# Attention inside a transformer block on TensorE: double units over two steps in place of single units over one

## The reference, cut to what is needed

```python
z = rms_norm(x, norm_mix_pre) @ w_in     # q 1024, k 128, v 128, q of memory 512, pooling 512, gates 3072 columns
# window attention: 16 heads of 64 in 2 groups of 8 that share k and v; a query chunk of 64 sees itself and the chunk before
s = einsum('bcqgrd,bckgd->bcgrqk', qb, kb) * 64 ** -0.5 + bias      # keys before the sequence: -1e30
p = softmax(concatenate([s, sink], -1), -1)[..., :-1]
o = einsum('bcgrqk,bckgd->bcqgrd', p, vb)
# memory attention: 4 heads of 128 over 256 memory tokens
s = einsum('bshd,bmhd->bhsm', q, mk) * 128 ** -0.5
o = einsum('bhsm,bmhd->bshd', softmax(s, -1), mv)
```

## Time and profile before

| | |
|---|---|
| median of three runs | 815.47 us |
| the profiled execution | 812.36 us, its span 810.6 us |
| TensorE matmuls busy | 799.6 us, 99% of the span |
| DVE busy | 463.4 us, 57% |
| ACT busy | 356.2 us, 44% |
| GpSimd busy | 45.4 us, 6% |

### The profile page before, as it was taken

How to read it: one execution, slowest core, us unless ns; L and a number is a source line. 1 busy time by engine, 2 the same in 40 slices (tenths; PEclk the granted TensorE clock), 3 DMA queues, 4 the chain that set the end, 5 groups by cost and what they waited for, 6 DMA issues and landing times.

```text
span 810.6 us, 11900 instructions
## 1 busy us (share of the span) xinstructions
PE 799.6 (99%) x4672; PEld 693.6 (86%) x4672; DVE 463.4 (57%) x624; ACT 356.2 (44%) x632; POOL 45.4 (6%) x100
## 2 busy tenths in 40 slices
PE   7999999999999999999999999999999999999997
PEld 6988777777788888888888899999999999888885
DVE  5742565566444432613755579888888887833222
ACT  6632545546444424224433455444444445632111
POOL 1100000144000000000001120000000000000000
PEclk9999999999999999999999999999999999999999
DMA  9543221211221322234462013333333334641011
GB/s 323 182 127 111 69 87 53 94 63 53 67 90 53 105 93 73 95 104 156 155 213 76 25 53 105 104 104 104 104 104 104 104 129 147 218 154 54 1 52 53
DMA packets 67786, 84.21 MB, mean 104 GB/s; under 512 B 3217, under 2 KB 61089, under 8 KB 67746
## 3 DMA queue, kind: packets, MB, share of 16 engines
q1 hardware_dynamic: 67712, 83.65, 30.9%
q10 hardware_dynamic: 34, 0.01, 0.0%
HBM read 81.54 MB, written 2.11 MB: 103 GB/s over the span
## 4 chain that ended last, share of the span: by engine, by line
PE 94%; DVE 3%; issue 1%; DMA 1%; POOL 1%; ACT 0%; SPq 0%; DVEq 0%; POOLq 0%; ACTq 0%
PE pair L1207 86%; PE pair L1299 1%; PE pair L1282 1%; PE pair L1309 1%; PE pair L1289 1%; PE pair L1214 1%; PE pair L1313 1%; DMA g_mem_b<-in_norm_mem 1%; POOL B_f L590 1%; DVE T_f L1094 1%; DVE op_lo L1074 1%; DVE T_lo L1101 0%; PE pair L1235 0%; DVE mem_in L873 0%; DVE sum_odd L1089 0%
## 5 line engine op out<-in xcount | busy, mean ns | idle before, releaser
L368 DVE TENSOR_TENSOR w_lo<-raw,w_hi 128x1024 fp32r<-128x1024 f32 x69 | 84.1, 1220 | 96.3 <-ACT w_hi L363 96.2
L1207 PE MATMUL pair<-hT_hi,w_hi 128*128 128x512 f32 x336 | 136.5, 406 | 0.0
L1207 PE MATMUL pair<-hT_lo,w_hi 128*128 128x512 f32 x336 | 131.3, 391 | 0.0
L1207 PE MATMUL pair<-hT_hi,w_lo 128*128 128x512 f32 x336 | 131.3, 391 | 0.0
L363 ACT ACTIVATE w_hi<-raw 128x1024 fp32r<-128x1024 f32 x70 | 73.9, 1055 | 89.3 <-PE pair L1207 86.4
L1207 PE MATMUL pair<-T_hi,op_hi 128*128 128x256 f32 x320 | 90.6, 283 | 0.5 <-DVE op_lo L1074 0.5
L1207 PE MATMUL pair<-T_lo,op_hi 128*128 128x256 f32 x320 | 90.6, 283 | 0.0
L1207 PE MATMUL pair<-T_hi,op_lo 128*128 128x256 f32 x320 | 90.6, 283 | 0.0
L1207 PEld LDWEIGHTS pair<-hT_hi,w_hi 128*128 128x128 f32 x336 | 63.1, 188 | 14.0
L1207 PEld LDWEIGHTS pair<-hT_hi,w_lo 128*128 128x128 f32 x336 | 63.1, 188 | 13.9
L1207 PEld LDWEIGHTS pair<-hT_lo,w_hi 128*128 128x128 f32 x336 | 63.2, 188 | 12.0
(11 more groups left out here) (185 smaller groups left out, 1578.6 us busy)
## 6 DMA issues: line engine op xcount, KB each, us to landing
raw<-in_w_in SPq DMA_DIRECT2D x42, 512.0 KB, 4.6
raw<-in_w_ffn_up SPq DMA_DIRECT2D x22, 512.0 KB, 4.7
raw<-in_w_ffn_gate SPq DMA_DIRECT2D x22, 512.0 KB, 4.7
raw<-in_w_ffn_down SPq DMA_DIRECT2D x22, 512.0 KB, 4.1
raw<-in_w_mem_kv SPq DMA_DIRECT2D x8, 512.0 KB, 7.0
raw<-in_w_branch_a SPq DMA_DIRECT2D x8, 512.0 KB, 4.0
raw<-in_w_out SPq DMA_DIRECT2D x8, 512.0 KB, 3.9
x_in<-in_x SPq DMA_DIRECT2D x4, 512.0 KB, 9.6
```

The costliest lines, as they stand in the source:

```text
L368: eng.tensor_tensor(lo, raw_view(s), hi.bitcast(F32), ALU.subtract).then_inc(weights_split, 1)
L1207: ins = pe.matmul(dst, a, b, start=first and n == 0, stop=last and n == 2, skip_group_check=onto)
```

## The change

Units are twice as large and half as many. A window unit has two neighbouring chunks, a memory unit a whole head with all 512 tokens: eight and four, twelve in all. Unit u belongs to the two steps from 15 + 2u. In the first (phase 0) come scores, maxima and exponentials, in the second (phase 1) the division, which now stands near the head of DVE's step, the turning after five eighths of the tile, and ACT's copy of the turned probabilities, which now stands behind its copies of the tiles before. The output is made at the head of the step after these two, ahead of the next unit's scores. The products are the same; a score matmul keeps its size, an output matmul of the window keeps its size, and one of the memory kind has 512 columns instead of two of 256. One set of probabilities remains (8 x 128 elements in a partition), and the turned ones are copied back over it. The turned probabilities take banks 6 and 7, the output takes bank 3, so weight tiles from step 13 to step 40 go round banks 0 to 2 and wait for the tile three before. DVE adds the bias in two operations for a double unit; each other operation of DVE and ACT there covers twice the elements, except the exponentials, which come one for each of 8 (or 4) rows of scores.

The diff, cut (the small vectors, the output's addresses and the parts of DVE that only widen are left out):

```diff
@@ -36,8 +36,8 @@
-A_UNITS = GROUPS * NC_
-X_UNITS = X_HEADS * 2
+A_UNITS = GROUPS * NC_ // 2
+X_UNITS = X_HEADS
@@ -151,8 +151,7 @@
-    probs = [sb(f"probs{i}", 112.5 + 2 * i, [P, 4, P]) for i in range(2)]
-    probsT = sb("probsT", 116.5, [P, 4, P])
+    probs = sb("probs", 112.5, [P, 8, P])
...
@@ -253,7 +252,19 @@
-        scores = pair[2]
+        scores, turned = pair[2], pair[3]
+        O_BANK = 3
+        bank_of, bank_before = [], {}
+        for n, t in enumerate(tiles):
+            step = next(i for i, end in enumerate(step_end) if n < end)
+            free = 3 if UNIT0 - 2 <= step <= UNIT0 + 2 * UNITS + 1 else 4
+            last = {b: m for m, b in enumerate(bank_of)}
+            b = min(range(free), key=lambda i: last.get(i, -1))
+            bank_of.append(b)
+            bank_before[n] = last.get(b)
+        last_in_o_bank = max(n for n, b in enumerate(bank_of) if b == O_BANK and n < step_end[UNIT0])
+        first_in_o_bank = min(n for n, b in enumerate(bank_of) if b == O_BANK and n >= step_end[UNIT0])
@@ -372,19 +383,27 @@
...
-                return "a", u // NC_, u % NC_
-            return "x", (u - A_UNITS) // 2, (u - A_UNITS) % 2
+                return "a", u // (NC_ // 2), u % (NC_ // 2)
+            return "x", u - A_UNITS, 0
+        def unit_at(step, phase):
+            u, r = divmod(step - UNIT0, 2)
+            return u if r == phase and 0 <= u < UNITS else None
...
@@ -616,27 +635,24 @@
-                if u >= 1:
-                    act.wait_ge(o_full, u)
-                act.activation(probsT[:, :, :], as4(bk(6)), ACT.Copy).then_inc(probsT_ready, 1)
+                act.activation(probs[:, :, :], turned[:, :, :].rearrange("p a (b k) -> p (a b) k", b=4), ACT.Copy)\
+                   .then_inc(probsT_ready, 1)
...
+                    for i in range(8):
+                        act.activation(probs[:, i, :], probs[:, i, :], ACT.Exp, bias=neg_max[:, i:i + 1],
+                                       accum_out=row_sum[:, i:i + 1])
+                    act.activation(sink_gap[:, :], sink_gap[:, :], ACT.Exp).then_inc(exps_done, 1)
+                else:
+                    flat = probs[:, :, :].rearrange("p (t m) k -> p t (m k)", t=4)
...
+                        at = N_MEM * (i % 2)
+                        ins = act.activation(flat[:, i, :], scores[:, i // 2, at:at + N_MEM], ACT.Exp,
+                                             bias=neg_max[:, i:i + 1], scale=X_SCALE, accum_out=row_sum[:, i:i + 1])
@@ -708,9 +724,8 @@
-                u = s - UNIT0
-                if 0 <= u - 2 < UNITS:
-                    o_hi(u - 2)
+                if unit_at(s - 2, 0) is not None:
+                    o_hi(unit_at(s - 2, 0))
@@ -718,8 +733,6 @@
-                if 0 <= u - 1 < UNITS:
-                    probsT_copy(u - 1)
@@ -729,8 +742,10 @@
-                if 0 <= u < UNITS:
-                    exps(u)
+                if unit_at(s, 1) is not None:
+                    probsT_copy(unit_at(s, 1))
+                if unit_at(s, 0) is not None:
+                    exps(unit_at(s, 0))
@@ -894,37 +916,36 @@
-                    if u >= 2:
-                        dve.wait_ge(probs_turned, u - 1)
-                    dve.scalar_tensor_tensor(out=pr[:, :, :].rearrange("p (a b) k -> p a b k", a=2),
-                                             in0=scores[:, :, 0:2 * KEYS].rearrange("p a (b k) -> p a b k", b=2),
-                                             scalar=A_SCALE,
-                                             in1=bias[:, a, :, :].rearrange("p (a b) k -> p a b k", a=2),
-                                             op0=ALU.mult, op1=ALU.add).then_inc(scores_read, 1)
-                    dve.wait_ge(scores_read, u + 1)
+                    for c in range(2):
+                        dve.scalar_tensor_tensor(out=probs[:, 4 * c:4 * c + 4, :].rearrange("p (a b) k -> p a (b k)", a=2),
+                                                 in0=scores[:, :, 2 * KEYS * c:2 * KEYS * c + 2 * KEYS], scalar=A_SCALE,
+                                                 in1=bias[:, a, :, :].rearrange("p (a b) k -> p a (b k)", a=2),
+                                                 op0=ALU.mult, op1=ALU.add).then_inc(scores_read, 1)
+                    dve.wait_ge(scores_read, 2 * u + 2)
...
+                        link(dve.memset(probs[:, 0:4, 0:CHUNK], -1e30))
+                    sinks_of = over_chunks(sink[:, :, :], 4 * a, 4)
+                    link(dve.tensor_reduce(row_max[:, :], probs[:, :, :], AX_X, ALU.max))
+                    link(dve.tensor_tensor(heads(row_max), heads(row_max), sinks_of, ALU.max))
+                    dve.tensor_tensor(heads(sink_gap), sinks_of, heads(row_max), ALU.subtract)
+                    dve.tensor_scalar(neg_max[:, :], row_max[:, :], -1.0, None, ALU.mult).then_inc(neg_max_ready, 1)
...
@@ -984,13 +1005,14 @@
-                u = s - UNIT0
-                if 0 <= u - 2 < UNITS:
-                    o_lo(u - 2)
+                if unit_at(s - 2, 0) is not None:
+                    o_lo(unit_at(s - 2, 0))
...
-                if 0 <= u < UNITS:
-                    maxima(u)
+                if unit_at(s, 0) is not None:
+                    maxima(unit_at(s, 0))
+                if unit_at(s, 1) is not None:
+                    normalise(unit_at(s, 1))
@@ -1023,8 +1045,6 @@
-                if 0 <= u < UNITS:
-                    normalise(u)
@@ -1223,9 +1243,11 @@
-                dst = bk(n % 4)
-                if n >= 4:
-                    before = tiles[n - 4]
+                dst = bk(bank_of[n])
+                if n == first_in_o_bank:
+                    pe.wait_ge(o_split, UNITS)
+                elif bank_before[n] is not None:
+                    before = tiles[bank_before[n]]
@@ -1265,38 +1287,43 @@
-                    if midway and k == ks[len(ks) // 2 - 1]:
+                    if midway and k == ks[5 * len(ks) // 8 - 1]:
...
-                    pe.wait_ge(scores_read if u <= A_UNITS else exps_done, u)
+                    pe.wait_ge(scores_read, 2 * min(u, A_UNITS))
...
+                if u > A_UNITS:
+                    pe.wait_ge(exps_done, u)
...
-                        ins = pe.matmul(scores[:, pr // 2, KEYS * (pr % 2):KEYS * (pr % 2) + KEYS],
-                                        q[lo:lo + 64, 2 * a + pr % 2, b, :, :].rearrange("p j t -> p (j t)"),
-                                        k_dup[lo:lo + 64, a, CHUNK * b:CHUNK * b + KEYS], start=True, stop=True)
+                        for c in range(2):
+                            at, ch = KEYS * (2 * c + pr % 2), 2 * b + c
+                            ins = pe.matmul(scores[:, pr // 2, at:at + KEYS],
+                                            q[lo:lo + 64, 2 * a + pr % 2, ch, :, :].rearrange("p j t -> p (j t)"),
+                                            k_dup[lo:lo + 64, a, CHUNK * ch:CHUNK * ch + KEYS], start=True, stop=True)
...
-                    for i in range(2):
-                        at = P * (2 * b + i)
-                        ins = pe.matmul(scores[:, i, 0:N_MEM], qx[:, a, at:at + P], mk[:, a, :], start=True, stop=True)
+                    for i in range(4):
+                        at = N_MEM * (i % 2)
+                        ins = pe.matmul(scores[:, i // 2, at:at + N_MEM], qx[:, a, P * i:P * i + P], mk[:, a, :],
+                                        start=True, stop=True)
...
-                for i in range(4):
-                    dst = i if u < A_UNITS else 2 * (i % 2) + i // 2
-                    ins = pe.transpose(bk(6)[:, P * dst:P * dst + P], probs[u % 2][:, i, :], ident[:, :])
+                for i in range(8):
+                    at = i if u < A_UNITS else 4 * (i % 2) + i // 2
+                    ins = pe.transpose(turned[:, at // 4, P * (at % 4):P * (at % 4) + P], probs[:, i, :], ident[:, :])
@@ -1304,13 +1331,18 @@
+                else:
+                    pe.wait_ge(tile_copied, copied_no[tiles[last_in_o_bank]])
...
-                    for half in range(2):
-                        ins = pe.matmul(bk(7)[64 * half:64 * half + 64, 0:2 * P], v_c[:, b, 64 * a:64 * a + 64],
-                                        probsT[:, 2 * half:2 * half + 2, :], start=True, stop=True)
+                    for c in range(2):
+                        for half in range(2):
+                            i = 4 * c + 2 * half
+                            ins = pe.matmul(bk(O_BANK)[64 * half:64 * half + 64, 2 * P * c:2 * P * c + 2 * P],
+                                            v_c[:, 2 * b + c, 64 * a:64 * a + 64], probs[:, i:i + 2, :],
+                                            start=True, stop=True)
...
-                        ins = pe.matmul(bk(7)[:, 0:2 * P], mv[:, m, a, :], probsT[:, 2 * m:2 * m + 2, :],
+                        ins = pe.matmul(bk(O_BANK), mv[:, m, a, :], probs[:, 4 * m:4 * m + 4, :],
@@ -1331,15 +1363,14 @@
-                u = s - UNIT0
-                if 0 <= u < UNITS:
-                    unit_scores(u)
```

(43 more changed lines are left out.)

30 lines of the change are left out of this document (7 added, 23 removed).

## The result

Over 20 runs of each, the kernel before has a median of 813.91 us (811.53 to 817.42) and the changed one 817.05 us (815.06 to 822.24). The ratio is 1.0043, 95% interval 1.0029 to 1.0057: slower by 3.1 us, where 2.2 us of gain was forecast. The 20 runs also put the kernel before 1.6 us under the three runs that the forecast was put on. Against 813.91 the same sum would have read 811.7, so the miss is 5.3 us. Two later executions, one of experiment 1 (2202 us) and one of experiment 2 (2825 us), were slow and are in no ratio.

A forecast was written before the change was run, and what follows sets the result against it. TensorE's stream was taken to bound the kernel, at full clock. Gain 5.3 less stalls 0.7 and 2.4 made 2.2 us, so 813.3 us from a median of 815.47; range 810.6 to 816.0, about 8 in 10.

The forecast's parts named there:

- Rival C: TensorE waits for late normalised probabilities before the turn in every double unit; 818.9 us if 1.5 us late; chance 0.07.
- Rival D: After the 2.4 us wait ahead of step 27 the clock halves, one tile costing another 5.4 us; 818.7 us; chance 0.02.
- Term 1: Window stage: 8 double units replace 16, so 0.66 us of changeover overhead is paid 8 times less; 5.3 us gained.
- Scores start 0.112 apart in their stream: Spacing of window score matmuls on TensorE, from which streaming of four scores was counted as 4 x 0.11 us.
- The lower bound of 4.4: Least gain from fewer window changeovers, if output matmuls keep 0.26 us and only part of the slow tile resumption goes.
- Term 4: Step 26: ACT's probabilities copy, now behind pin tile 3 and map tile 0, stalls step 27's outputs 2.4 us.
- Term 3: Fifth window unit, steps 23 and 24: DVE's small maxima operations wait for GpSimd's pooling; 0.7 us of stall.
- Term 2: A double unit's DVE and ACT chain fits in two steps, margin 0.8 us; no stall in a plain unit.
- rival E: Joined groups cost the same, the 0.66 us being per matmul; the 5.3 us gain goes to 0; 818.6 us; chance 0.02.
- the sign that was named for E: A plain window double step of 14.8 us without a wait, where the forecast had 14.2 us.
- In the first unit there is no output group, which pays for the bias copy: First window unit: the missing outputs were taken to offset the bias copy against the 0.8 us margin.
- Memory units and the ring of three banks: Halving memory units counted at zero (upper bound 0.2 us); bank waits covered by a full tile, otherwise 0.6 us a step.

The follow-up runs named there:

- experiment 1: Changed kernel with the double unit's score matmuls issued chunk by chunk instead of all lower rows first; median 813.71 us, ratio 0.999 to the kernel before.
- experiment 2: Changed kernel with ACT's copy of the turned probabilities put ahead of its tile copies, pin tile 3 included; 813.11 us, ratio 0.9996 to the kernel before.
- 6: Changed kernel with scores issued chunk by chunk and lower and upper row half in turn; 812.85 us, ratio 0.9981 to the kernel before.
- experiment 5: Changed kernel with a third buffer for the copied pin tiles, ACT's copy order left alone; 813.16 us, ratio 0.999 to the kernel before.
- Experiment 7: Changed kernel with chunk-by-chunk scores, probabilities copied first, and the turn after six eighths in units 0 and 4; 809.01 us, ratio 0.9947 to the kernel before.
- 3: Changed kernel with nine throwaway 512-column matmuls filling TensorE's wait ahead of step 27's outputs; 815.37 us, ratio 1.0023 to the kernel before.
- 4: Changed kernel with scores chunk by chunk and ACT's copy of the turned probabilities first; 810.21 us, ratio 0.9958 to the kernel before.
- 8: Changed kernel with row halves in turn, probabilities copied first, and the later turn in units 0 and 4; 808.99 us, ratio 0.9941 to the kernel before.
- 9: The kernel of 8 with 48 instead of 30 idle-time matmuls at the start; 807.72 us, ratio 0.9917 to the kernel before.

## Why the prediction was wrong

The measured time lies outside the range, on the side of the rivals C and D but by a way that none of them named in full.

**Term 1 failed, and with it the sign.** "Scores start 0.112 apart in their stream" is true of pairs: in the earlier trace rows the count falls by two, from x6 to x4, between starts 0.12 apart, one pass on each row half. The forecast doubled the pairs and took it for granted that the pairing stays. But the diff makes the chunk the inner loop and so puts the four matmuls of one half together, and that had to be read as part of the change. It costs 8 x (1.64 - 1.10) = 4.3 us of the 5.3 us; experiments 1 and 6 gave back 3.6 and 4.4 by the groups, 3.4 and 4.1 by the stage. The rest of the term was right and slightly low: with the scores at 1.10 the double step would have been 14.69 - 0.54 = 14.15 us, a gain of 0.72 against 0.66, which over eight is 0.5 more (with the halves in turn 14.11 to 14.13 was measured). The lower bound of 4.4 for the term did not hold this case, because it was made of the outputs' and the tile's resumption only.

**Rival D was dismissed on too little.** It named the mechanism that came: half clock after the stall of Term 4. Against it stood that an idle time of 2.5 us at the start left the clock at full. That was one execution; in others of this study an idle time of 1.3 to 3.0 us at the same place is followed by half clock (last section). A case that one execution shows to be possible is not shown to be the rule. The price of D was 5.4 us for a whole tile; it was 1.6, because the clock came back within 4 us. As a term of the forecast, and not a rival, it would have been right at a third of its size. The Trainium skill, page TensorE: Matmul & The Clock Gate, section on HAM oscillation in real kernels, spoke for it with longer waits, and the trace agrees with it in kind: 0.50 granted after the wait.

**Term 4 was right.** One wait ahead of step 27's outputs, of 2.2 us where 2.4 was forecast, released by ACT's copy, which stood behind pin tile 3 and map tile 0. GpSimd and DVE met as foreseen. GpSimd in its second group, then DVE's product and weight split beside it:

```profile
163.78 3.02 POOL L592 TENSOR_TENSOR pooled<-pooled 128x512 f32<-128x512 f32 x2 [17.89 <-PE pair L1257]
166.89 1.47 POOL L596 TENSOR_SCALAR pooled<-pooled 128x512 f32<-128x512 f32 x1
...
168.72 1.29 POOL L598 TENSOR_TENSOR pooled<-pooled,pooled 128x512 f32<-128x512 f32 x1
```

```profile
163.95 1.95 DVE L948 TENSOR_TENSOR probs<-probs,inv_denom 128x1024 f32<-128x1024 f32 x1
165.82 2.06 DVE L379 TENSOR_TENSOR w_lo<-raw,w_hi 128x1024 fp32r<-128x1024 f32 x1
```

GpSimd's group lasted 6.2 us from 163.78 (5.44 before); 6.5 was reckoned. The product took 1.95 us and the split 2.06, where each takes 1.22 to 1.23 away from GpSimd's work. The rows read as turns: GpSimd's second add, from 164.90 to 166.80, took 1.90 where the first took 1.04, and it ends 0.9 us after the product does (165.90). Experiments 2 and 5 show the whole chain: take away either the order or the buffer and the wait is gone. The rule that the prediction took from the Trainium skill, page SBUF — State Buffer, section on the two separate sides (both meetings paid in full, 2.5), was nearer than the undisturbed rows (0.6).

**Term 3 was right in kind.** A wait in step 24, of 0.28 us plus slower matmuls around it: the double step took 15.18 us against 14.69, 0.5 more, where 0.7 was forecast. The meeting was with the small operation one place earlier than expected, the maximum with the sinks; the usual 0.17 us became 1.00:

```profile
144.91 1.00 DVE L929 TENSOR_TENSOR row_max<-row_max,sink 128x8 f32<-128x8 f32 x1
```

**Term 2 was right but for unit 0.** In the plain unit shown above the product ends at 104.71 + 1.23 = 105.94 and TensorE wants it at 106.78: a margin of 0.8 us, as reckoned.

```profile
104.71 1.23 DVE L948 TENSOR_TENSOR probs<-probs,inv_denom 128x1024 f32<-128x1024 f32 x1
```

Rival C and rival E fall with that (waits in two units of twelve, and 14.11 us for the double step once the order is mended). The changed kernel's 14.69 us without a wait came close to the sign that was named for E, 14.8; the order of the scores, and not a price per matmul, was behind it. "In the first unit there is no output group, which pays for the bias copy" was false. TensorE's and DVE's times in the unit both count from its scores; the outputs ahead of them delay both alike. The bias copy (0.70) and the memset (0.27) therefore use up the margin, and TensorE waited 0.2 us and lost 0.4. Experiment 7 moved the turn and got the 1.1 us of both units back.

**Memory units and the ring of three banks** cost and gained nothing, as reckoned: 15.27 and 15.30 us for a double step against 15.32 for two steps before, and no wait for a bank in the list.

The sum with the measured terms: forecast -2.2; scores +4.3; clock +1.6; unit 0 +0.4; unit 4 -0.2; wait in step 27 -0.2; changing over -0.5. That is +3.2, and 3.2 was measured in the stage.

## What to carry to other kernels

When a group of small matmuls that use half the rows of the array grows, look at the order in which the halves are issued (1.64 against 1.09 us for eight here). Reading "the spacing of starts" needs the number of passes that start together, and the diff's loop order belongs to the costs. A wait of TensorE of some 2 us should be priced with the clock behind it, as a term (1.6 us here) and not as a remote case; if the wait can't be removed, throwaway matmuls in it give that part back. And a copy that the bottleneck waits for stands ahead of copies that may be held by a slow engine.

## What the runs showed of the hardware that was not expected

- **The clock after a wait.** A TensorE wait of 2.2 us, up to 172.2, was followed by matmuls at full clock up to 174.0 and then by some 3.4 us at 1.2 GHz in the changed kernel. In experiments 1 and 6 the same wait was followed by 0.8 and 1.5 us at full clock and then 3.4 us at 1.2 GHz. With the wait filled (3) or gone (2, 4, 5, 7, 8) the clock stayed at 1.00 there.
- **The clock near the start varies from run to run.** Behind the idle time ahead of the first memory rows (L1234), the profiled executions of 1, 2, 4, 6, 8 and 9 had the slice from 15.0 to 17.5 us at 0.50 to 0.60. Here is 4, whose idle time was 1.5 us:

```profile
15.00:17.50 2.50, 2.50 (x14) 2.50 (x13) 1.98 (x3) 2.50 (x3) 0.00 (x0) 0.50 1.02 408
17.50:20.00 2.50, 2.50 (x20) 2.50 (x20) 1.78 (x2) 0.56 (x3) 0.80 (x2) 0.86 1.06 331
```

  In the kernel before, the changed one and 3, 5 and 7 the same slices read 1.00, with idle times of 1.6 to 2.6 us; in the six others these were 1.3 to 3.0. The length of the idle time does not decide it, and what does is open. The clock goes with the spread between the runs of a kernel: of the 31 runs of the kernel before beside experiment 1, the seven with a mean granted clock of 0.999 took 812.0 to 812.6 us and the two with 0.992 took 817.4 and 817.5. That is the reason why the stage, and not the run, was compared above.
- **The wait for a held buffer was laid to TensorE.** The view names the semaphore that came last by its own reckoning; only the earlier end of the named work (and experiment 5) told that it was GpSimd.
